# GpSimd weights heads 2 and 3 of every attention step in one product, VectorE weights heads 0 and 1

## The reference, cut to what matters

```python
p_s = masked_softmax(s_s, mask_s)                 # branch b = 0, selected
o_s = jnp.einsum("bgrtm,bgtmd->bgrtd", p_s, gv)
p_w = masked_softmax(s_w, mask_w)                 # branch b = 1, window
o_w = jnp.einsum("bgrtk,bgkd->bgrtd", p_w, vw)
o = gates[..., 0:1] * o_c + gates[..., 1:2] * o_s + gates[..., 2:3] * o_w
```

## Time and profile before

| | |
|---|---|
| median of 3 runs | 2590.38 us (2585.9 to 2591.2) |
| profiled execution | 2590.4 us, span 2588.6 us |
| TensorE busy | 2524.0 us, 98% |
| VectorE busy | 1243.3 us, 48% |
| GpSimd busy | 1255.5 us, 48% |
| ScalarE busy | 904.0 us, 35% |
| chain that ended last | PE 89%, DVE 7%, ACT 1%, POOL 1% |

### The profile page before, as it was taken

How to read it: one execution, slowest core, us unless ns; L and a number is a source line. 1 busy time by engine, 2 the same in 40 slices (tenths; PEclk the granted TensorE clock), 3 DMA queues, 4 the chain that set the end, 5 groups by cost and what they waited for, 6 DMA issues and landing times.

```text
span 2588.6 us, 34392 instructions
## 1 busy us (share of the span) xinstructions
PE 2524.0 (98%) x11696; PEld 2044.5 (79%) x11696; DVE 1243.3 (48%) x1471; ACT 904.0 (35%) x1278; POOL 1255.5 (48%) x879
## 2 busy tenths in 40 slices
PE   8999999999999999999999999999987799999998
PEld 7887788888888888877888888887755587888887
DVE  6434612452322552443135322257797844788363
ACT  5223333332222332343234322233355433444233
POOL 5555255555555554534565545555422343555454
PEclk9999999999999999999999999999998899999999
DMA  5332133333333333312333333363211131333332
GB/s 161 97 96 83 57 101 94 98 98 98 98 96 98 92 97 97 97 58 86 93 97 98 98 98 98 97 151 96 74 50 50 49 90 52 94 97 97 97 96 76
DMA packets 448118, 236.22 MB, mean 91 GB/s; under 512 B 16144, under 2 KB 442256, under 8 KB 447888
## 3 DMA queue, kind: packets, MB, share of 16 engines
q1 hardware_dynamic: 446896, 232.38, 31.2%
q10 hardware_dynamic: 1120, 2.51, 0.3%
HBM read 232.76 MB, written 2.10 MB: 91 GB/s over the span
## 4 chain that ended last, share of the span: by engine, by line
PE 89%; DVE 7%; issue 1%; ACT 1%; POOL 1%; DMA 0%; DVEq 0%; POOLq 0%; ACTq 0%
PE unit_ps L1678 59%; PE unit_ps L1799 16%; PE unit_ps L1785 7%; PE aux L1713 2%; PE o_banks L1743 1%; DVE a_f L1353 1%; DVE c_f L1221 1%; DVE row L1339 1%; PE aux L1731 1%; POOL wl L422 1%; PE aux L2026 1%; PE unit_ps L1713 0%; PE unit_ps L2086 0%; DVE aux L1337 0%; PE aux L2044 0%
## 5 line engine op out<-in xcount | busy, mean ns | idle before, releaser
L422 POOL TENSOR_TENSOR wl<-raw,wh 128x512 fp32r<-128x512 f32 x862 | 1249.0, 1469 | 1313.1 <-ACT wh L499 839.9
L499 ACT ACTIVATE wh<-raw 128x1024 fp32r<-128x1024 f32 x304 | 323.2, 1063 | 1030.9 <-PE unit_ps L1678 971.1
L1678 PE MATMUL unit_ps<-ah,wh 128*128 128x512 f32 x1280 | 502.9, 393 | 3.6 <-DVE tmp L1078 3.6
L1678 PE MATMUL unit_ps<-ah,wl 128*128 128x512 f32 x1280 | 498.9, 390 | 0.0
L1678 PE MATMUL unit_ps<-al,wh 128*128 128x512 f32 x1280 | 498.7, 390 | 0.0
L1678 PE MATMUL unit_ps<-bh,wh 128*128 128x512 f32 x768 | 299.7, 390 | 0.0
L1678 PE MATMUL unit_ps<-bh,wl 128*128 128x512 f32 x768 | 298.8, 389 | 0.0
L1678 PE MATMUL unit_ps<-bl,wh 128*128 128x512 f32 x768 | 298.8, 389 | 0.0
L1678 PEld LDWEIGHTS unit_ps<-ah,wh 128*128 128x128 f32 x1280 | 240.7, 188 | 55.8 <-DVE tmp L1078 4.4
L1678 PEld LDWEIGHTS unit_ps<-al,wh 128*128 128x128 f32 x1280 | 240.6, 188 | 51.4 <-issue 1.9
L1678 PEld LDWEIGHTS unit_ps<-ah,wl 128*128 128x128 f32 x1280 | 240.7, 188 | 50.2
(11 more groups left out here) (349 smaller groups left out, 3856.1 us busy)
## 6 DMA issues: line engine op xcount, KB each, us to landing
raw<-w_in_dram SPq DMA_DIRECT2D x147, 512.0 KB, 4.0
raw<-w_up_dram SPq DMA_DIRECT2D x64, 512.0 KB, 4.0
raw<-w_down_dram SPq DMA_DIRECT2D x64, 512.0 KB, 4.0
raw<-up_dram SPq DMA_DIRECT2D x44, 512.0 KB, 3.8
raw<-w_conv_out_dram SPq DMA_DIRECT2D x16, 512.0 KB, 4.1
raw<-w_ret_out_dram SPq DMA_DIRECT2D x16, 512.0 KB, 3.8
raw<-w_o_dram SPq DMA_DIRECT2D x16, 512.0 KB, 3.9
raw<-down_dram SPq DMA_DIRECT2D x16, 512.0 KB, 3.8
```

Source lines behind the costliest of these rows:

```text
L422: last = pool.tensor_tensor(wl[j][:, half], raw[j % 2][:, half], wh[j][:, half].bitcast(F32), ALU.subtract)
L499: act.activation(wh[j][:], raw[j % 2][:], ACT.Copy).then_inc(w_hi, 1)
L1678: last = pe.matmul(unit_ps[j % 2][:], w[j][:, k], v[:, k * T:(k + 1) * T], start=(k == 0 and n == 0), stop=(k == KB - 1 and n == 2))
```

## The change

Two semaphores are new. `w_att` is signalled by VectorE when the weights of a step (gate / sum) are ready; `p_pool` is signalled by GpSimd when its product is done. GpSimd's loop over the units is cut in three, and for the 20 units around the attention stage it is written out. Behind the two subtractions of unit MK + 4 + k GpSimd waits for `w_att` and multiplies heads 2 and 3 of step k, two rows of nk elements, by their weights in one product whose second operand is a broadcast of one number per head. VectorE multiplies heads 0 and 1 only. TensorE waits for `p_pool` as well as `p_ready` ahead of `first_turns(k)`. VectorE waits, from k = 2 on, for the product of step k - 2, since it overwrites the row of weights that this product reads.

```diff
+        w_att, p_pool = sem("w_att"), sem("p_pool")
@@ gpsimd
-            units(pool, U_END // 4 * 4, body)
+            def weigh(k):
+                it, b, c, rp = STEPS2[k]
+                pool.wait_ge(w_att, k + 1)
+                p = p_att[k % 3][:, 2:REP, 0:(c + 1) * P]
+                pool.tensor_tensor(p, p, row[:, 4 * b + 3, 2:REP].unsqueeze(2).broadcast_to([P, 2, (c + 1) * P]), ALU.mult).then_inc(p_pool, 1)
+
+            att_from, att_to = (MK + 4) // 4 * 4, (MK + 4 + N_STEPS + 3) // 4 * 4
+            units(pool, att_from, body)
+            for u in range(att_from, att_to):
+                body(u, u % 4)
+                if 0 <= u - MK - 4 < N_STEPS:
+                    weigh(u - MK - 4)
+            units(pool, U_END // 4 * 4 - att_to, lambda u, j: body(u + att_to, j))
@@ vector, weigh(k)
                 dve.wait_ge(exp_att, REP * (k + 1))
+                if k >= 2:
+                    dve.wait_ge(p_pool, k - 1)
                 go()
                 did(dve.reciprocal(row[:, 4 * b + 3], row[:, 4 * b + 1]))
                 at = NSA_HEADS * (1 + b) + REP * rp
-                mult(row[:, 4 * b + 3], row[:, 4 * b + 3], gates[:, c, at:at + REP])
-                for h in range(REP):
+                mult(row[:, 4 * b + 3], row[:, 4 * b + 3], gates[:, c, at:at + REP], w_att)
+                for h in range(2):
                     go()
                     p = p_att[k % 3][:, h, 0:nk]
-                    did(dve.tensor_scalar(p, p, row[:, 4 * b + 3, h:h + 1], None, ALU.mult), p_ready if h == REP - 1 else dve_step)
+                    did(dve.tensor_scalar(p, p, row[:, 4 * b + 3, h:h + 1], None, ALU.mult), p_ready if h else dve_step)
@@ tensor, first_turns(k)
                 pe.wait_ge(p_ready, k + 1)
+                pe.wait_ge(p_pool, k + 1)
```

## The result

The changed kernel takes 2594.78 us (median of 13 runs, 2590.24 to 2598.89), the kernel before 2590.98 (13 runs, 2585.9 to 2593.18). The ratio is 1.0018, with an interval of 1.0011 to 1.0026: slower, by about 4.7 us, and on the edge of the 0.2% that this kernel's measurement can tell. The forecast was 2599.6 with a range of 2590 to 2610. The time lies in the range, but it is that of rival 1 (2591.5 to 2595.5). The profiled execution of the changed kernel is one of its slower ones, 2597.26 us with a span of 2595.5, against 2590.4 and 2588.6 before. So what follows counts 6.9 us in the spans where the medians differ by 3.8, and its stage is 7.5 us longer.

What follows compares the result with a forecast made beforehand. It took VectorE as the bound from 1907 to 1946 us and no engine as full from 1959 us on. Tail 7.7 + VectorE's shift 0 + clock 1.5 = 9.2 us, on 2590.4 gives 2599.6, range 2590 to 2610.

Steps and rivals of the forecast that it cites:

- rival 1: VectorE's gain up to step 9 gets through, as products meet few taps or cost half: 2591.5 to 2595.5 us, chance 0.20.
- The ring by place: Steps 12 to 15: TensorE's first transposes wait for GpSimd's product behind its subtractions; intervals 8.28 to 10.68 us, excess 10.45.
- Even with a product at no cost: Steps 12 to 15: the excess from the product's place behind the subtractions alone, 7.6 us or so.
- The cover at the end: End of the stage: VectorE, still scaling x, takes the last values 2.75 us late, which hides that much; 7.7 left.
- Steps 1 to 8: Shorter steps stretch to the ring, step 7's first transposes some 5 us late; TensorE's 4.64 us idling at step 9 swallows it.
- The shift of VectorE at step 9: How much earlier or later VectorE reaches step 9: zero taken, bounds -5 and +4 us.
- the balance of 8.5 us gained and 9 lost: VectorE up to step 8: 8.5 us of weightings removed, 9 lost if half the products meet its taps; nothing left.
- The price of the product: GpSimd's new product: 2.34, 1.80, 1.26 and 0.72 us by size, bounds half and one and a half times.
- The clock: TensorE idles more in the tail, and a lower clock lengthens memory units: 1.5 us, bounds 0 and 5.
- the holding: Steps 0 to 8: time GpSimd's products could hold off VectorE's taps, 17.9 us in all.
- The port: Port shared by VectorE and GpSimd: a tap meeting the largest product is held for that product's whole length.
- The likeliest case: The forecast itself, 2599.6 us with its own range 2596 to 2605, chance 0.60.

Runs made afterwards that it cites:

- eight matmuls in the wait: The changed kernel with 8 extra 128x128 matmuls on TensorE in the first transposes of steps 11 to 15, ahead of the wait for GpSimd: 2593.96 us, ratio 1.0011.
- thin product: The changed kernel with GpSimd's product cut to 2 x 8 elements in every step, place and waits unchanged: 2587.82 us, ratio 0.9988.
- relief alone: The changed kernel without GpSimd's product and the two waits for it, heads 2 and 3 weighted by nobody: 2580.61 us, ratio 0.9960.
- with full operands: The changed kernel with GpSimd multiplying heads 2 and 3 by a full operand in another tile in place of the weights: stage 175.7 us, no median given.
- the kernel with twelve: The changed kernel with 12 extra 128x128 matmuls on TensorE in the first transposes of steps 11 to 15, before the GpSimd wait: 2593.38 us, ratio 1.0011.

## Why the prediction was right or wrong

- **The ring by place: right.** FT waits for L431. With eight matmuls in the wait the excess is 35.0 - 25.9 = 9.1 us, where 10.45 were worked out from the earlier trace rows; on either side the unit of step 15 alone is at the low clock (4.62 us, before 4.13). At the full clock the intervals are 8.47, 8.49 and 8.09 for the forecast's 8.72, 8.71 and 8.28; 0.11 of the difference is the product's, 0.61 for 0.72. "Even with a product at no cost" 7.6 would be left: thin product against relief alone gives 6.6 us by the medians and 8.3 by the stages, the latter with some of the clock in it.
- **The cover at the end: right.** 2.75 us were taken off, and now `take_out(7)` starts 0.08 us behind the last values (2040.91), which take 0.44 us longer from FT(15) on at the low clock. So FT(15), later by 14.4 - 4.7 = 9.7, leaves 7.5 in the stage.
- **Steps 1 to 8: right in kind.** FT(7) was to be some 5 us late and the wait of 4.64 to swallow it. FT(7) is 4.4 us late, the wait is down to 1.00.
- **The shift of VectorE at step 9: wrong, 0 taken, -5.0 measured.** This term is the step that failed, and it lay at the bound that was given for it. Two things in it were wrong. First, the balance of 8.5 us gained and 9 lost: VectorE's weightings and taps of steps 0 to 8 take 51.5 us before (23.2 and 28.3) and 39.3 after (9.7 and 29.6), 12.3 less and not about the same. The product holds off weightings or taps in steps 0 to 3 only. And the stalls that the subtractions had caused before, which the balance left out, are mostly gone from step 4 on (in steps 4 to 7 the taps took 3.21 to 4.24 us before and take 2.33 after), since GpSimd's pair now comes so late that it hardly meets VectorE's taps. Second, FT(8) doesn't move "with VectorE alone". In steps 3 to 7 TensorE waits for the product (0.46 to 2.01 us) and VectorE for TensorE, so the ring takes back a part: FT(8) is 9.6 us early with the thin product, 5.0 with the whole one. The price acts through the ring and not through the port: with full operands VectorE's weightings and taps take 38.8 us, as little as with the weights, and still FT(8) is only 0.2 early, in part for the low clock of that execution.

```profile
1932.10 2.32 DVE L1236 SCALAR_TENSOR_TENSOR c_f<-hp,vectors,c_f 128x512 f32<-128x512 f32 x3
1937.21 0.43 DVE L1352 TENSOR_TENSOR aux<-aux,diag 128x256 f32<-128x256 f32 x1 [2.79 <-PE aux L1919]
```

  This is step 5. The three taps take what they take alone, where they took 3.21 before the change, and VectorE stands idle 2.79 us for TensorE's scores (L1919): the ring binds.
- **The price of the product: 1.89, 1.47, 1.04 and 0.61 for 2.34, 1.80, 1.26 and 0.72.** The bound "half" was given for the reason that a repeated number isn't read each time. A repeated operand is cheaper, but by 15 to 19%.
- **The clock: mis-sized.** 1.5 us taken with bounds 0 and 5; 5.3 between the two profiled tails, beyond the bound. In the medians the extra matmuls gained 1.2 and 0.1 us only, so its size there stays open.
- **The sum.** 7.7 + 0 + 1.5. By the profiles it is 9.1 for the ring, -2.2 for the cover (2.67 less 0.44), -4.7 at FT(11), +5.3 for the clock: 7.5, which is the stage's. The two terms that were furthest off, the shift and the clock, have opposite signs and nearly cancel in the profiled execution, so its nearness to 9.2 is luck. Some slips in the recorded working change nothing in it: the holding sums to 17.8 and not 17.9, VectorE has one new wait and not two, and in rival 1 one of the two conditions alone gives 7.7 - 5 = 2.7 or 7.7 - 1.4 = 6.3, not "to 5".
- **The port.** The first product took 1.89 us, and the two weightings that met it 2.74 in place of the 1.01 of step 1 (half of 2.05 in the earlier trace rows): 1.73 of 1.89 us lost. The Trainium skill, page "SBUF — State Buffer", section "SBUF: two separate sides", has the loser blocked for the whole instruction; the trace agrees in the blocking, here for a product of 1.89 us. The section gives the ports to the one that starts first, which this row doesn't bear out: by the profile the weighting started 0.04 us ahead of the product (1879.63 and 1879.67) and was the one held.

```profile
1879.63 2.74 DVE L1370 TENSOR_SCALAR a_f<-a_f,row 128x512 f32<-128x512 f32 x2
```

- **The chances.** The likeliest case had 0.60, rival 1 had 0.20 and came out. It was said to decide at a shift of -4 at step 9, and it did. But of its sum only the 5 us at step 9 came as written: the 1.4 of a product at half price is 0.4 (4 x 0.11), and it has no term for the clock. That the median lies in its range is in part luck. The range 2590 to 2610 holds the measured time only because it was drawn around rival 1 too; the forecast's own 2596 to 2605 doesn't.

## What to carry to other kernels

Before work is handed to an engine with room, ask what stands ahead of it there: here the product stood behind a step of another chain that started from the work which waited for the product, and that ring cost about 7 us by the medians even with the product cut to a few columns. The same move pays where the steps are longer than the ring (0.20% faster in steps 0 to 8 alone) and costs where they are shorter (0.41% slower in steps 12 to 15 alone), so a place and a range of steps have to be chosen for each. And an engine that shares a port with the one that is relieved should start when the other doesn't need it, not at the same signal.

## What was not expected of the hardware

GpSimd's product of two float32 operands took 1.04 us for 128x512 when the second operand repeats one number per row or is the first operand again, and 1.27 when it lies in another tile (0.43 against 0.54 us for each 256 elements). The Trainium skill, page "GPSIMD Engine Reference", section "Elementwise — side-by-side cycle accounting", gives one figure of about 2.6 cycles an element for two inputs and a measured 4497 ns for an addition of 2048 elements, which is 0.56 us for each 256, an estimate; the trace agrees for operands in two tiles (0.54), and differs for these (0.43). Why a square is cheap too wasn't tried. The 128x128 matmuls added to the wait took 0.25 us each (twelve in 2.95), where transposes of that size come at 0.14 (eight in 1.09). In the timeline of the kernel with twelve each of these matmul calls stands as two records, each transpose as one.

```profile
2008.33 2.94 PE L1971 MATMUL unit_ps<-mean_d 128*128 128x128 f32 x24
```
